# The order of two groups of products in the gate stage, and of the output tiles in the last ff tile

## What is computed

```
x = x + (silu(gate) * val) @ w_down                  # 2816 ff features to 1024
g = sigmoid(_rmsnorm(x, norm3) @ w_ple_gate + b_ple_gate)
x = x + (p @ w_ple_proj) * g                          # p: 512 x 256, w_ple_proj: 256 x 1024
return _rmsnorm(x, final_norm)
```

## Time and profile before

| | |
|---|---|
| median of 3 runs | 1328.21 us |
| the profiled execution's own time | 1323.81 us |
| its span on the core | 1322.0 us |
| TensorE busy with matmuls | 1267.3 us, 96% |
| VectorE, ScalarE, GpSimd busy | 750.7, 463.9, 162.5 us |
| matmuls of the down stage (GHL), each of three lines | 352, some 390 ns |
| matmuls with XH or XL, each of three lines | 1096, some 397 to 402 ns |

### The profile page before, as it was taken

The page is one execution under the profiler, slowest core; times in us unless marked ns, Lnnn a source line. Parts: engine busy times, 40 slices in busy tenths (PEclk is TensorE's granted clock), DMA queues, the critical chain, the costliest instruction groups (busy, mean ns, idle before and its releaser), DMA issues.

```text
span 1322.0 us, 15810 instructions
## 1 busy us (share of the span) xinstructions
PE 1267.3 (96%) x5487; PEld 980.6 (74%) x5487; DVE 750.7 (57%) x1107; ACT 463.9 (35%) x744; POOL 162.5 (12%) x139
## 2 busy tenths in 40 slices
PE   6899699999999999999999999999999999999996
PEld 4687455555488878888888888888778888888885
DVE  5538776677546856455554545454533366347665
ACT  4311455555512333332223232322232234225333
POOL 0137400000045500000000000000000011002100
PEclk9899799999999999999999999999999999999999
DMA  5410000010153312222222222222244444443332
GB/s 180 176 49 18 10 10 1 10 31 1 35 204 96 112 49 80 79 64 79 64 79 63 79 63 79 63 79 63 85 153 144 145 145 147 147 138 96 103 119 88
DMA packets 116108, 113.39 MB, mean 86 GB/s; under 512 B 6291, under 2 KB 98794, under 8 KB 115306
## 3 DMA queue, kind: packets, MB, share of 16 engines
q1 hardware_dynamic: 115776, 112.84, 27.0%
q10 hardware_dynamic: 298, 0.11, 0.0%
HBM read 93.01 MB, written 19.92 MB: 85 GB/s over the span
## 4 chain that ended last, share of the span: by engine, by line
PE 80%; DVE 6%; issue 1%; ACT 1%; DMA 0%; DVEq 0%; SPq 0%; ACTq 0%
PE ps L189 25%; PE ps L191 25%; PE ps L190 25%; PE ps L524 3%; PE ps L512 2%; DVE XT L1240 1%; DVE SF L1217 1%; DVE XT L1220 1%; DVE XT L1216 1%; DVE col L1233 0%; DMA SF<-g_scratch 0%; DVE WDHL L1226 0%; DVE TL L1461 0%; DVE GHL L1228 0%; PE ps L707 0%
## 5 line engine op out<-in xcount | busy, mean ns | idle before, releaser
L189 PE MATMUL ps<-XH,WH 128*128 128x512 f32 x1096 | 440.7, 402 | 3.7 <-DVE SF L1132 3.7
L190 PE MATMUL ps<-XL,WH 128*128 128x512 f32 x1096 | 434.9, 397 | 0.0
L191 PE MATMUL ps<-XH,WL 128*128 128x512 f32 x1096 | 434.9, 397 | 0.0
L202 DVE TENSOR_TENSOR WL<-WR,WH 128x1024 fp32r<-128x1024 f32 (+2 forms) x137 | 174.2, 1274 | 190.2 <-ACT WH L197 190.1
L197 ACT ACTIVATE WH<-WR 128x1024 fp32r<-128x1024 f32 (+2 forms) x137 | 139.6, 1020 | 327.7 <-PE ps L191 319.4
L189 PEld LDWEIGHTS ps<-XH,WH 128*128 128x128 f32 x1096 | 208.1, 190 | 55.3 <-DVE WL L202 4.6
L190 PEld LDWEIGHTS ps<-XL,WH 128*128 128x128 f32 x1096 | 208.2, 190 | 49.3 <-issue 2.2
L191 PEld LDWEIGHTS ps<-XH,WL 128*128 128x128 f32 x1096 | 208.0, 190 | 48.6
L965 ACT ACTIVATE SF<-SF,col 128x512 f32<-128x512 f32 x88 | 71.7, 816 | 300.6 <-DVE SF L1335 300.5
L1335 DVE TENSOR_TENSOR SF<-ps,R 128x512 f32<-128x512 f32 x88 | 60.5, 689 | 180.8 <-PE ps L191 175.2
L189 PE MATMUL ps<-GHL,WH 128*128 128x512 f32 x352 | 137.3, 390 | 2.7 <-DVE GHL L1378 1.9
(11 more groups left out here) (151 smaller groups left out, 1252.1 us busy)
## 6 DMA issues: line engine op xcount, KB each, us to landing
WR<-in_w_up SPq DMA_DIRECT2D x44, 512.0 KB, 3.8
WR<-in_w_down SPq DMA_DIRECT2D x44, 512.0 KB, 3.6
g_scratch<-SF SPq DMA_DIRECT2D x22, 512.0 KB, 2.9
SF<-g_scratch SPq DMA_DIRECT2D x44, 256.0 KB, 3.7
WR<-in_w_out SPq DMA_DIRECT2D x16, 512.0 KB, 3.7
WR<-in_w_ple_gate SPq DMA_DIRECT2D x16, 512.0 KB, 3.6
WR<-in_w_in SPq DMA_DIRECT2D x8, 512.0 KB, 3.8
xt_scratch<-XT SPq DMA_DIRECT2D x2, 2048.0 KB, 13.0
```

Of the source, the lines that this page charges most:

```text
L189: pe.matmul(out, wh, xh, start=first, stop=False)
L190: pe.matmul(out, wh, xl, start=False, stop=False)
L191: return pe.matmul(out, wl, xh, start=False, stop=last)
L202: dve.tensor_tensor(WL[:, slot(n), base:cols, :], WR[:, slot(n), base:cols, :], WH[:, slot(n), base:cols, :].bitcast(F32), ALU.subtract).t ...
```

## The change

Three things. In a gate tile the PLE products are issued ahead of the gate products, each group with its own waits. The last ff tile of group 1 goes through the banks in the order 4, 0, 2, 1, 5, 3, 6, 7 (`LAST_M`), and so do the eight additions behind it; counts of `dn_free` are translated with `LAST_M.index`. The first two PLE weight loads and splits go ahead of the first two gate weight loads and splits, on SyncE, ScalarE and VectorE.

```diff
+LAST_M = [4, 0, 2, 1, 5, 3, 6, 7]
...
+            for k in range(2):
+                ple_load(k)
             for k in range(NSEQ * KT):
                 gate_load(k)
-                ple_load(k)
+                if k >= 2:
+                    ple_load(k)
...
-                for m in range(KT):
+                for m in LAST_M if last and s else range(KT):
...
                 n, c = T_GATE + k, k % 2
+                pe.wait_ge(pl_lo, k + 1)
+                if k >= 2:
+                    pe.wait_ge(gp_ready, k - 1)
+                else:
+                    pe.wait_ge(dn_free, KT + LAST_M.index(4 + c) + 1)
+                for a in range(2):
+                    ins = mm3(pe, ps[4 + c][:, :], PLH[:, c, a, :], PLL[:, c, a, :],
+                              PH[:, a, s, :], PL[:, a, s, :], a == 0, a == 1)
+                ins.then_inc(ple_ready, 1)
                 pe.wait_ge(w_lo, n + 1)
                 if k >= 2:
                     pe.wait_ge(gz_ready, k - 1)
                 else:
-                    pe.wait_ge(dn_free, KT + c + 1)
+                    pe.wait_ge(dn_free, KT + LAST_M.index(c) + 1)
                 for a in range(KT):
                     if m == 0:
                         pe.wait_ge(x3_lo, s * KT + a + 1)
                     ins = mm3(pe, ps[c][:, :], WH[:, slot(n), a, :], WL[:, slot(n), a, :],
                               XH[:, s, a, :], XL[:, s, a, :], a == 0, a == KT - 1)
                 ins.then_inc(gate_ready, 1)
-                pe.wait_ge(pl_lo, k + 1)
-                if k >= 2:
-                    pe.wait_ge(gp_ready, k - 1)
-                else:
-                    pe.wait_ge(dn_free, KT + 4 + c + 1)
-                for a in range(2):
-                    ins = mm3(pe, ps[4 + c][:, :], PLH[:, c, a, :], PLL[:, c, a, :],
-                              PH[:, a, s, :], PL[:, a, s, :], a == 0, a == 1)
-                ins.then_inc(ple_ready, 1)
...
             def add_down(k):
                 s, m = divmod(k, KT)
+                m = LAST_M[m] if s else m
...
+            for k in range(2):
+                ple_hi(k, None, 0)
             ring_hi(T_GATE, 0, dn_tile, 2 * (FT - 1))
             ring_hi(T_GATE + 1, 0, dn_ready, 2 * KT)
...
-            for k in range(2):
-                ple_hi(k, dn_ready, 2 * KT)
             copy_r(B_X3, 3)
...
+            for k in range(2):
+                ple_low(k)
             split_w_lo(dve, T_GATE, T_GATE)
             for m in range(KT):
                 add_down(KT + m)
             split_w_lo(dve, T_GATE + 1, T_GATE + 1)
...
-            for k in range(2):
-                ple_low(k)
             norm3(0)
```

More of the change, by code:

```diff
@@ L709, in turn_x4 @@
                         ins.then_inc(f_tr, 1)
-            pe.wait_ge(dn_free, KT + 3)
+            pe.wait_ge(dn_free, KT + LAST_M.index(2) + 1)
             pe.wait_ge(sq_sum, 16 + KT)
@@ L1003, in x3_hi_of @@
                 s, m = divmod(k, KT)
-                act.wait_ge(dn_free, k + 1)
+                act.wait_ge(dn_free, s * KT + (LAST_M.index(m) if s else m) + 1)
                 act.activation(XH[:, s, m, :], xt[:, s, m, :], ACT.Copy,
@@ L1027, in _, with ple_hi @@
                 down(1, q * 2, 1)
+            def ple_hi(k, free, count):
+                act.wait_ge(ple_in[k % 2], 16 * (k // 2 + 1))
+                if count:
+                    act.wait_ge(free, count)
+                act.activation(PLH[:, k % 2], PLR[:, k % 2], ACT.Copy).then_inc(pl_hi, 1)
+            for k in range(2):
+                ple_hi(k, None, 0)
             ring_hi(T_GATE, 0, dn_tile, 2 * (FT - 1))
             ring_hi(T_GATE + 1, 0, dn_ready, 2 * KT)
[L1032 to L1036, removed]
             def gate(k):
@@ L1416, in _, with ple_low @@
                 down_lows(q * 2, FT + 1)
+            def ple_low(k):
+                dve.wait_ge(pl_hi, k + 1)
+                dve.tensor_tensor(PLL[:, k % 2], PLR[:, k % 2], f32(PLH[:, k % 2]), ALU.subtract).then_inc(pl_lo, 1)
+            for k in range(2):
+                ple_low(k)
             split_w_lo(dve, T_GATE, T_GATE)
@@ L1420, in _ @@
             split_w_lo(dve, T_GATE + 1, T_GATE + 1)
-            def ple_low(k):
-                dve.wait_ge(pl_hi, k + 1)
-                dve.tensor_tensor(PLL[:, k % 2], PLR[:, k % 2], f32(PLH[:, k % 2]), ALU.subtract).then_inc(pl_lo, 1)
             def gate(k):
```

## The result

The changed kernel takes 1331.26 us, the median of 20 runs (1325.67 to 1335.65), against 1328.23 us for the kernel before in as many runs: +3.0 us. The ratio is 1.0023, with a 95% interval of 1.0013 to 1.0034. Forecast were 1330.9 us and a ratio of 1.0020.

A forecast was written before the change was run, and what follows sets the result against it. From 1150 us to the end of tile 15 TensorE's gapless matmuls bound the kernel, then the last chain and norm. Terms 1.4 (last chain) + 1.3 (tile 14) + 0 = 2.7 us on 1328.2 gave 1330.9 us, range 1327.8 to 1333.2.

The forecast's parts named there:

- The entry: Start of the gate stage: TensorE waits for nothing there; reordered banks, splits and loads cost and gain 0.
- The tile pattern: Ordinary gate tiles: gate products end 1.4 us later, PLL keeps 1.6 us in reserve, so no stall.
- The collision in tile 2: Rival: PLL of tile 2 slowed beside GpSimd's addition, 1.1 us more, 1332.0 us; 17% with like waits in other tiles.
- Tile 14: TensorE waits at tile 14's start for PLL, its weights requested behind the fourth output store: 1.3 us, bounds 0.4 to 2.1.
- the late load that does not bite: Rival: tile 14's weights land nearer 3.6 us, so the wait is 0.4 us or less; 1329.8 us, 18%.
- The last chain: After tile 15: GZ, sigmoid, product, addition, transposes and norm follow the last gate product later, 1.4 us.
- The pace of the matmuls: Rival: in gate tiles the new order speeds matmuls from 0.232 to 0.227 us, winning 2.7 us; 1328.2 us, 10%.
- The clock: TensorE's clock: the 1.3 us wait in tile 14 was given no cost, as 1.00 followed a wait before the transposes.
- my own list of signs: Expected profile: new wait near 1294 of 1.2 to 1.4 us; wait at the transposes grows from 1.7 to some 3.
- the likeliest case: The forecast of 2.7 us slower, 50%, spanning 1329.3 to 1332.3 us.
- the parts named for the chances: Shares of each case behind the chances: slower by more than 0.2% 0.49, within 0.44, faster 0.07.

The follow-up runs named there:

- e_entry_only: Changed kernel with gate products first again in all 16 gate tiles, leaving only the bank order and earlier PLE loads and splits: ratio 1.0002.
- h_both: Changed kernel with gate tile 15 in the old order and tile 14's loads issued between the second and third output store: ratio 1.0008.
- a_early: Changed kernel with the loads for gate tile 14 issued between the second and third output store instead of behind the fourth: ratio 1.0004.
- c_tile15_old: Changed kernel with gate tile 15 alone in the old order, gate products first: ratio 1.0003.
- b_tile15_new: Kernel before with gate tile 15 alone in the new order, PLE products first: ratio 1.0015.
- after_again2: Changed kernel traced once more without edit: 139.7 us from the first bank addition to the end; no ratio.
- d_busy: Changed kernel with 11 extra matmuls, results unused, on TensorE in the wait ahead of the final transposes: ratio 1.0004.
- i_early_split: Changed kernel with tile 14's loads between the stores and 16 of the last 32 transposes moved ahead of tile 15's last addition: ratio 0.9992.

## Why the prediction was right, and where it was not

- **The entry: 0.** Right. TensorE did not wait there, and e_entry_only has the starts of the kernel before.
- **The tile pattern: no stall in ordinary tiles.** Right: no wait in tiles 0 to 13, and h_both is at 120.18 us. The collision in tile 2 did not come; PLL took 0.42 us at 1207.99, as before, with the PLE products of tile 2 at 1208.60.
- **Tile 14: 1.3 us.** Right in place, cause and size: 1.26 us in the starts, 1.24 by a_early, which takes it out, and 1.40 by c_tile15_old, which keeps only it (121.60 against 120.20). The loads took as long as before (4.5 to 5.0 us to land, against 4.5 to 5.3 in the earlier trace rows; VectorE's WL came 1.4 us later against the additions), so the late load that does not bite fell.
- **The last chain: 1.4 us.** Right: 1.36 us in b_tile15_new, 1.43 in a_early, 1.27 in c_tile15_old, which has the last six matmuls beside the chain again.
- **The pace of the matmuls.** Fell: from GZ of tile 4 to GZ of tile 5 it is 6.97 us still (1229.69 to 1236.66 in the changed kernel), and h_both has 120.18 us against 120.20.
- **The clock: no cost.** Wrong, and it is the one step that failed. I took the 1.7 us of wait in the trace of before, with 1.00 behind it, as evidence for the new one of 1.3 us in tile 14, and there it held (1.00 from 1297 to 1304 us in the trace). But by my own list of signs the wait ahead of the transposes was to grow to some 3 us, and for that length no row spoke. It cost 1.2 us in the first trace. By the Trainium skill ("TensorE: Matmul & The Clock Gate", section "Why this matters for your kernels") idle gaps between bursts of matmuls bring TensorE back to half its clock. The traces agree in five of six cases of 3.1 us, with 0.50 for 3.4 us or more, and show no fall in four cases of 1.7 us. Four are few: in after_again2 the clock fell 2.0 us behind the last matmul, only 0.3 us later than a wait of 1.7 us would have ended. That a wait of 1.7 us is always free is not shown.
- **Two slips without weight.** By its own terms the likeliest case starts at 1329.5 and not at 1329.3 (1.8 us more, less the half), and the parts named for the chances add up to some two hundredths more than 1.

The terms of the forecast add to 2.67 us in the trace, as forecast, and with the clock to 3.9 (3.6 and 4.1 in the two repeats). The timed difference of 3.0 us (1.7 to 4.5 by the interval) holds both sums, so the time does not decide between them; the traces do.

The total span differs by 3.6 us more than that, since the additions start later. They start anywhere from 1183.7 to 1194.0 us in the thirteen traces. The three traces of the changed kernel lie at 1190.0, 1191.3 and 1194.0, those of before and of e_entry_only at 1186.4, which looks like a cost of the change. But d_busy and i_early_split do the same work as the changed kernel up to this point and start the additions at 1186.35 and 1183.71, and if it were a cost, the timed medians would have to differ by 7 us or more, and they differ by 3.0. Of the 3.6 us between the two traces, 1.4 lie between VectorE's first split of GHL and the first down matmul. That stretch takes 351.8 us in before (595.8 to 947.6) and 353.2 in the changed kernel (598.1 to 951.3), but 351.8 also in d_busy (595.7 to 947.5) and 353.2 in b_tile15_new (595.0 to 948.2), which has the code of before there. In each of the thirteen traces it is 351.7 to 351.8 or 353.2 to 353.3 us, whichever the kernel. Why there are two values stays open.

## What to carry to other kernels

When two groups of work on the bottleneck engine are swapped, look at the last tile: the one that stands last there decides which is hidden under the closing chain, so what the chain waits for goes first and what it does not goes last. Then follow what each group waits for into the tile that is supplied late, here by a load queued behind stores; a wait that used to be met 24 matmuls later is now met at once. And when a change lengthens a wait of TensorE, ask for evidence at the new length: what a wait of 1.7 us did not cost in four traces, one of 3.1 us did in five of six. In the two traces where that wait was filled, once with useful transposes and once with matmuls for nobody, the clock stayed up.

## What the runs showed of the hardware that was not expected

- The clock's fall is not the same from one execution to the next: behind the same wait of 3.06 us, 3.50 for the weight loads, the weight loads of the 32 transposes took 3.48, 4.93, 5.10, 5.14, 5.14 and 6.27 us, and the fall came 2.0 to 3.9 us behind the last matmul. The same page of the Trainium skill (section "What's actually happening") says that the number of slow matmuls at a kernel's start varies from run to run; here the like shows behind a wait near the end.
- The first matmul behind a wait costs 0.34 us to the next start instead of 0.23, in tile 14 of the changed kernel. Its weight load starts together with it, at 1298.61, where the next one starts 0.24 us ahead of its matmul (1298.71 to 1298.95). Behind the sums of squares, where the weight load is 0.03 us ahead (1190.10 to 1190.13), it is 0.32 us. That the late weight load is the reason fits both, but was not tested by a run.
- The end of this kernel is noisy by less than 0.1 us as long as the clock stays (GZ to last scalings 9.62 or 9.63 in six traces), while the 1186 us before the additions vary by 10 us. A change of 1 us is seen within a stage and not in the total.
